# Decode attention on cached pages: fp32 products for four sequences at once on four column groups, in place of split fp32r products one sequence at a time

## The chip, the cores and the metric

The kernel runs on one core of one Trainium2 chip. The metric is the device time of one execution in microseconds (us), the median of several executions. Engines: PE is TensorE's matmul, PEld its weight load, DVE is VectorE, ACT is ScalarE, POOL is GpSimd, SP is SyncE; q behind a name (PEq, SPq) is that engine's queue.

## The reference, cut to what matters

One layer of a hybrid decoder, for a prompt of 2048 positions and for 8 sampled tokens (8 sequences, one new position each, behind 2048 cached positions in pages of 128). The part that is changed is the attention of the 8 sampled tokens over their caches:

```python
def mla_attend(q_abs, q_r, q_pos, ckv, kr, k_pos):
    s = (jnp.einsum('bqhr,bkr->bhqk', q_abs, ckv).astype(jnp.float32)
         + jnp.einsum('bqhp,bkp->bhqk', q_r, kr).astype(jnp.float32)) * SOFTMAX_SCALE
    mask = q_pos[:, None] >= k_pos[None, :]
    s = jnp.where(mask[None, None], s, NEG_INF)
    p = jax.nn.softmax(s, axis=-1).astype(ckv.dtype)
    return jnp.einsum('bhqk,bkr->bqhr', p, ckv)
...
        past_ckv = cache_ckv[l][page_table].reshape(dec_b, past_len, KV_RANK)
        past_kr = cache_krope[l][page_table].reshape(dec_b, past_len, QK_ROPE)
        xs, c_s, k_s, s_s = mixer_layer(xs, past_len, state_pool[l], past_ckv, past_kr, *lw)
```

Here b is 8 sequences, h 8 heads, q one query, k 2048 cached keys and the new one; a latent key (`ckv`, 128 numbers) is also the value, a rotary key (`kr`) has 64 numbers. Everything is float32.

## The kernel before

The program is four stages, each a block that ends when all engines are through: `project` (latents, keys and queries of 17 tiles of 128 positions, the last tile being the sampled tokens), `attend` (the prompt's causal attention, 32 units of 4 heads by 128 queries), `decode` (the sampled tokens' attention) and `merge` (gates and output products, in 5 chunks of 412 tokens). Nothing of one stage runs in another, except what `early_decode` holds: tiles and semaphores that `attend` fills for `decode`.

The prompt's products are made with fp32r operands, each number as a high part (rounded to fp32r) and a low part (the rest), and three products in place of one: high·high, high·low, low·high (L108, and `PARTS` at L911). The high part is an ACT copy, the low part a DVE subtraction (`split`, L78, whose instructions all carry L80).

**In attend.** The order of the instructions of PE, ACT and DVE is planned by `attend_orders` (L504) and is the same list before and after. Ahead of that list DVE makes the row numbers of the cache's pages (L761), clears `q` and `qp_f` (L763, L764), waits for the loads of the decode queries and copies them to `qc_f` and, one group of 8 columns for each sequence in a row of zeros, to `qp_f` (L766, L770). ACT makes their high parts ahead of its first exponential (L733, L734), DVE the low parts ahead of its first normalisation, step P of unit 0 (L814, L815). When POOL has split the last queries it issues the indirect loads of the caches of sequences 0 and 1 (L715; `fetch_cache`, L887).

**In decode.** POOL issues the other six sequences' loads at once, latent cache `cn` (1 MB each) and rotary cache `rn` (0.5 MB) in turn. There are 32 steps, one for each sequence s and each quarter c of its keys (512 keys):

- PE turns four 128x128 tiles of latent keys and two of rotary keys (two 64-number keys side by side) into PSUM with an identity (L1024, L1027);
- ACT copies them out as high parts (L960, L961), DVE subtracts them for the low parts (L980, L982);
- PE makes the scores of the step before (L1008, L1012): 3 + 6 products. The stationary operand is 64 columns wide, with the 8 heads of sequence s in their place and zeros elsewhere, so that all 8 sequences add up in one bank of 64 rows per quarter.

Then follow, one behind the other: the new key's scores (L1038, L1040), five evictions to `sc` with their maxima (L985, L989), one exponential over 64 rows by 2056 (L963), the reciprocal (L995), the normalisation (L997), 17 transposes (L1048, L1050), evictions to `pt` (L965, L999), and the values: for each sequence 17 plain fp32 products with 8 stationary columns (`pt`) and 128 moving ones (the latent cache), L1057 and L1059. PE turns the result (L1064), ACT evicts it, SP stores it (L946), and the block ends.

A plain fp32 product is one instruction of the program and shows as two MATMULs and two LDWEIGHTS in the trace; fp32r products and transposes show as one each.

Of the kernel before, what the change touches and what calls it, by code (L numbers as in the profile page):

```python
# [27 lines left out]
P = 128  # L28
# [3 lines left out]
NDEC = 8  # L32
# [27 lines left out]
SH = NDEC * NH  # L60
SROW = SH + NH
RUN = PAST // P
EARLY = 2
# [549 lines left out]
def attend(nc, io, keep, early):  # L613
# [3 lines left out]
    with ExitStack() as ctx:  # L617
# [3 lines left out]
        def sem(name):  # L621
# [26 lines left out]
        pages, run, rows, q, qc_f, qp_f, qc, qp = (  # L648
            early[name] for name in ("pages", "run", "rows", "q", "qc_f", "qp_f", "qc", "qp"))
        pages_in, rows_ok, dq_in, q_zero, qc_f_ok, qp_f_ok, dq_hi, dq_ok = (  # L650
            early[name] for name in ("pages_in", "rows_ok", "q_in", "q_zero", "qc_f_ok", "qp_f_ok", "q_hi", "q_ok"))
# [49 lines left out]
        def _(pool):  # L701
# [13 lines left out]
            for sequence in range(EARLY):  # L715
                fetch_cache(pool, io, rows, sequence, early["cn"][sequence], early["rn"][sequence],
                            early["cache_in"][sequence])

        @block.scalar
        def _(act):  # L720
            for step in orders["ACT"]:
# [7 lines left out]
                elif kind == "E":  # L729
                    if step == ("E", 0, 0, 0):  # L730

                        act.wait_ge(qp_f_ok, 1)
                        act.activation(qp[:, 0, :, :], qp_f[:, :, :], ACT.Copy).then_inc(dq_hi, 1)  # L733
                        act.activation(qc[:, 0, :, :], qc_f[:, :, :], ACT.Copy).then_inc(dq_hi, 1)  # L734
# [23 lines left out]
        def _(dve):  # L758
# [5 lines left out]
            dve.memset(qp_f[:, :, :], 0.0).then_inc(q_zero, 1)  # L764
            dve.wait_ge(dq_in, 80)
            dve.tensor_copy(qc_f[:, :, :].rearrange("p a (s h) -> p a s h", s=NDEC),  # L766
                            q[:, :, :, :].rearrange("p a h s -> p a s h")).then_inc(qc_f_ok, 1)
            dve.wait_ge(qc_f_ok, 1)
            dve.wait_ge(q_zero, 2)
            dve.tensor_copy(qp_f[:, :, :].rearrange("p a (s c) -> p a s c", s=NDEC)[:, :, :, 0:NH],  # L770
                            qc_f[:, :, :].rearrange("p a (s h) -> p a s h", s=NDEC)).then_inc(qp_f_ok, 1)
            dve.wait_ge(mask_in, 16)
            for step in orders["DVE"]:
# [35 lines left out]
                elif kind == "P":  # L809
                    if step == ("P", 0, 0, 0):  # L810

                        dve.wait_ge(qp_f_ok, 1)
                        dve.wait_ge(dq_hi, 2)
                        split(dve, qp[:, 1, :, :], qp_f[:, :, :], qp[:, 0, :, :]).then_inc(dq_ok, 1)  # L814
                        split(dve, qc[:, 1, :, :], qc_f[:, :, :], qc[:, 0, :, :]).then_inc(dq_ok, 1)  # L815
# [79 lines left out]
def decode(nc, io, keep, early):  # L895
# [5 lines left out]
    with ExitStack() as ctx:  # L901
# [100 lines left out]
        def _(pe):  # L1002
# [14 lines left out]
            for n in range(STEPS):  # L1017
                s, c = n // 4, n % 4
                if c == 0:
                    pe.wait_ge(cache_in[s], 32)  # L1020
# [721 lines left out]
```

## Time and profile before

| | |
|---|---|
| median of 3 runs | 2333.02 us (2332.59 to 2333.3) |
| the profiled execution, its own time | 2344.84 us |
| its span, first to last instruction | 2343.0 us |
| PE busy, share of the span | 2205.3 us, 94% |
| PEld, DVE, ACT, POOL | 87%, 56%, 43%, 16% |
| HBM read, written | 213.45 MB, 42.79 MB |
| project | 0 to about 250 us |
| attend | about 250 to 944 us |
| decode | 949.0 (first instruction of PE) to 1072.1 us (store issued) |
| merge | from 1079.3 us to the end |

Times on the trace are microseconds from the span's start. The windows view gives for each stretch what each engine was busy, with the number of instructions, the mean clock granted to TensorE as a share of 2.4 GHz (0.50 is 1.2 GHz), and the load of the DMA engines. The timeline view merges neighbouring instructions of a kind (x4 is four) and gives in brackets the idle time ahead of them and who ended it. A matmul's own duration holds its way through the array, so back-to-back matmuls are measured by the distance of their starts, not by their durations.

### The profile page before, as it was taken

Reading aid. Unit: us, or ns where it says so; the run is one execution under the profiler, and the core shown is the slowest. Engines: PE = TensorE matmul, PEld = TensorE weight load, DVE = VectorE, ACT = ScalarE, POOL = GpSimd, SP = SyncE. Lnnn points to the kernel's source line nnn. Section 1 sums busy time; section 2 is a strip of 40 time slices with the busy share of each in tenths; the row PEclk is TensorE's granted clock in tenths of the full one; section 3 lists DMA queues with packets and bytes.
Section 4 is the critical chain, followed back from the end, with each engine's and each line's share of the span. In section 5 each row is a group of like instructions: output and inputs, shape, how many; then the busy total and the mean of one; then the engine's idle time right before and its main releaser. Section 6 shows DMA issues by size and latency. Waiting matters only on the chain.

```text
span 2343.0 us, 33629 instructions
## 1 busy us (share of the span) xinstructions
PE 2205.3 (94%) x12021; PEld 2036.9 (87%) x12021; DVE 1308.4 (56%) x2647; ACT 1002.9 (43%) x1802; POOL 364.7 (16%) x500
## 2 busy tenths in 40 slices
PE   5999599999999998786999999999999999999997
PEld 4888478888888887665999999999999999999997
DVE  4565477788777776332644455444644464446445
ACT  3555456555555544322433343334333443344333
POOL 1333221111000010101400050004100420023001
PEclk9999799999999999887999999999999999999999
DMA  5454432111110010404453434443453345344533
GB/s 171 150 162 145 118 81 55 41 35 34 28 28 28 19 64 5 166 1 156 129 176 119 142 118 157 145 137 119 135 166 121 128 136 174 106 150 134 175 117 131
DMA packets 134866, 257.99 MB, mean 110 GB/s; under 512 B 18682, under 2 KB 84482, under 8 KB 133430
## 3 DMA queue, kind: packets, MB, share of 16 engines
q1 hardware_dynamic: 111454, 223.29, 29.3%
q10 hardware_dynamic: 20960, 20.19, 2.9%
q0 software_dynamic: 2304, 12.58, 1.4%
q8 instruction: 88, 1.44, 0.3%
q14 instruction: 60, 0.49, 0.1%
HBM read 213.45 MB, written 42.79 MB: 109 GB/s over the span
## 4 chain that ended last, share of the span: by engine, by line
PE 51%; DVE 1%; issue 1%; DMA 0%; ACT 0%; POOL 0%; DVEq 0%; POOLq 0%; SPq 0%; ACTq 0%
PE d_ps L112 50%; PE d_ps L1567 1%; DMA d_hf<-out_ht 0%; DVE d_gate_p L1518 0%; DVE d_mrg L80 0%; POOL d_fstat L1389 0%; DVE d_y L1481 0%; ACT d_mrg L1347 0%; ACT d_zs L1375 0%; DVE d_ya L1522 0%; DVE d_ht L80 0%; ACT d_ht L1293 0%; DVE d_pool L80 0%; DVE d_y L1556 0%; DVE d_y L1483 0%
## 5 line engine op out<-in xcount | busy, mean ns | idle before, releaser
L112 PE MATMUL d_ps<-d_ht,d_wr 128*128 128x412 f32 x3840 | 737.4, 350 | 22.2 <-DVE d_ht L80 22.1
L112 PEld LDWEIGHTS d_ps<-d_ht,d_wr 128*128 128x128 f32 x3840 | 718.3, 188 | 26.2 <-issue 22.6
L80 DVE TENSOR_TENSOR d_wr<-d_ws,d_wr 128x1024 fp32r<-128x1024 f32 x262 | 322.9, 1232 | 553.4 <-ACT d_wr L1288 553.3
L1288 ACT ACTIVATE d_wr<-d_ws 128x1024 fp32r<-128x1024 f32 x262 | 277.5, 1059 | 608.2 <-PE d_ps L112 598.9
L842 PE MATMUL b_ps<-kt,b_qs 128*128 128x512 f32 (+3 forms) x1600 | 359.8, 377 | 18.6 <-POOL b_qs L80 13.8
L842 PEld LDWEIGHTS b_ps<-kt,b_qs 128*128 128x128 f32 x1600 | 278.3, 195 | 65.2 <-POOL b_qs L80 14.3
L861 PE MATMUL b_ps<-b_pt,kv 128*128 128x512 f32 x816 | 211.5, 402 | 8.7 <-DVE b_pt L80 8.7
L80 DVE TENSOR_TENSOR b_pt<-b_ps,b_pt 128x512 fp32r<-128x512 f32 x272 | 171.9, 683 | 83.0 <-ACT b_pt L746 82.6
L739 ACT ACTIVATE b_p<-b_p,b_bias 128x1024 f32<-128x1024 f32 (+7 forms) x192 | 172.0, 898 | 103.8 <-DVE b_low L797 100.4
L746 ACT ACTIVATE b_pt<-b_ps 128x512 fp32r<-128x512 f32 x272 | 143.8, 596 | 146.6 <-PE b_ps L852 146.3
L861 PEld LDWEIGHTS b_ps<-b_pt,kv 128*128 128x128 f32 x816 | 153.6, 191 | 48.3 <-DVE b_pt L80 14.1
L112 PE MATMUL d_ps<-d_mrg,d_wr 128*128 128x412 f32 x960 | 188.8, 352 | 0.7
L112 PE MATMUL d_ps<-d_gat,d_wr 128*128 128x412 f32 x960 | 186.5, 349 | 0.0
L112 PEld LDWEIGHTS d_ps<-d_gat,d_wr 128*128 128x128 f32 x960 | 179.5, 188 | 0.6
L112 PEld LDWEIGHTS d_ps<-d_mrg,d_wr 128*128 128x128 f32 x960 | 175.8, 188 | 3.7 <-DVE d_mrg L80 2.4
L80 POOL TENSOR_TENSOR b_qs<-b_qf,b_qs 128x512 fp32r<-128x512 f32 x64 | 87.9, 1373 | 519.1 <-ACT b_qs L728 516.5
L852 PE MATMUL b_ps<-ident,b_p 128*128 128x128 f32 x1088 | 137.6, 275 | 14.6 <-DVE b_p L820 14.3
L852 PEld LDWEIGHTS b_ps<-ident,b_p 128*128 128x128 f32 x1088 | 125.7, 142 | 29.1 <-DVE b_p L820 16.9
L790 DVE TENSOR_SCALAR_CACHE_REDUCE b_p<-b_ps 128x512 f32<-128x512 f32 x192 | 130.6, 686 | 35.7 <-PE b_ps L842 27.8
L1411 POOL TENSOR_TENSOR d_win<-d_u 128x426 f32<-128x426 f32 x20 | 21.2, 1062 | 740.8 <-ACT d_u L1330 740.0
L820 DVE TENSOR_SCALAR b_p<-b_p,b_inverse 128x1024 f32<-128x1024 f32 (+7 forms) x192 | 122.9, 670 | 1.4
L112 PE MATMUL a_ps<-a_wlat,a_ht 128*128 128x448 f32 x408 | 89.0, 374 | 6.5 <-DVE a_wlat L80 6.5
(193 smaller groups left out, 2289.4 us busy)
## 6 DMA issues: line engine op xcount, KB each, us to landing
d_ws<-in_w SPq DMA_DIRECT2D x264, 512.0 KB, 3.5
out_q<-a_qout SPq DMA_DIRECT2D x17, 768.0 KB, 3.3
d_hf<-out_ht SPq DMA_DIRECT2D x26, 412.0 KB, 3.5
a_x<-in_x ACTq DMA_DIRECT2D x17, 512.0 KB, 3.8
out_ht<-a_hf SPq DMA_DIRECT2D x17, 512.0 KB, 4.2
d_olf<-out_olat SPq DMA_DIRECT2D x42, 206.0 KB, 2.9
b_qf<-out_q SPq DMA_DIRECT2D x32, 256.0 KB, 2.8
b_qf<-out_q SPq DMA_DIRECT2D x128, 64.0 KB, 2.6
```

The lines of the kernel that those rows point to most:

```text
L80: return e.tensor_tensor(low, source, high.bitcast(f32), ALU.subtract)
L112: mm = pe.matmul(out, stationary(a, k), moving(b, k), start=first and k == 0 and a + b == 0, stop=last and k == depth - 1 and a == 1)
L739: act.activation(sp_[row][:, keys], sp_[row][:, keys], ACT.Exp, bias=bias[:, row:row + 1], scale=SCALE, accum_out=total[:, row, part:part ...
L746: act.activation(pt[n % NPT][:, 0, :], ps_t[n % NTB][:, :], ACT.Copy).then_inc(pt_hi, 1)
L790: dve.tensor_scalar(out, inp, 1.0, None, ALU.mult, ALU.max, accum_out=top[:, row, c:c + 1]).then_inc(s_sb, 1)
L820: dve.tensor_scalar(sp_[row][:, keys], sp_[row][:, keys], inverse[:, row:row + 1], None, ALU.mult).then_inc(p_ok, 1)
L842: mm = pe.matmul(ps_s[n % NS][:, 0:keys * P], q[:, a, h, :], kt[:, first:first + keys, b, :], start=k == 0, stop=k == len(pairs) - 1)
L852: mm = pe.transpose(ps_t[n % NTB][:, h * P:h * P + P], sp_[(u % 2) * HG + h][:, j * P:j * P + P], ident[:, :])
L861: mm = pe.matmul(ps_o[u % 2][:, :], kv[:, j, a, :], pt[n % NPT][:, b, :], start=j == 0 and k == 0, stop=j == tiles(u) - 1 and k == 2)
L1288: act.activation(wr[k % 2][:, 0, :, :], ws[k % 4][:, :, :], ACT.Copy).then_inc(w_hi, 1)
L1411: own(pool.tensor_tensor(out[:, start:HIST + T], source[:, start:HIST + T], source[:, start - shift:HIST + T - shift], ALU.add))
L1567: mm = pe.transpose(bank[xt_bank(n)][0:rows, s * P:s * P + P], yt[n % 2][:, s * P:s * P + rows], ident[:, :])
```

## The change

`decode` is written anew; `early_decode` and a few steps of `attend` change with it.

- **Products.** Queries (`qd`) and keys are plain fp32, no high and low parts. The queries of each sequence stand in 32 stationary columns (8 heads, 24 zeros; `PAD`).
- **Four sequences at once.** A step is one quarter of the keys of four sequences, 8 steps in all. Sequence j of the four writes rows 32j to 32j+31 of the same bank. The calls go round the four sequences: four products of 512 columns, then twice four of 256. The same rows and the same going round hold for the new key's scores and for the values, which have 32 stationary columns now.
- **Copies.** ACT copies the latent keys out of PSUM, DVE the rotary keys, each once. Three banks for turned latent keys, two for rotary.
- **Softmax.** One for each four sequences, over 128 rows. The exponentials are not normalised; the values are, when they are evicted. Of the first four it is placed under the steps of the second four.
- **Memory and loads.** `ckeys` lies where attend's `kv` was. Latents of four and rotary keys of three sequences are loaded in attend (was two and two); decode loads rotary keys 3 first, then four sequences' of both less one.
- **Unchanged:** the reference's outputs, attend's planned order, the other stages.

The core of the diff (the evictions of the softmax and the declarations are left out):

```diff
-EARLY = 2
+QUAD = 4
+PAD = P // QUAD
+EARLY_N, EARLY_R = 4, 3
...
@@ attend, vector, ahead of the planned order @@
-            dve.memset(qp_f[:, :, :], 0.0).then_inc(q_zero, 1)
+            dve.memset(qd[:, :, :, :], 0.0).then_inc(q_zero, 1)
             dve.wait_ge(dq_in, 80)
-            dve.tensor_copy(qc_f[:, :, :].rearrange("p a (s h) -> p a s h", s=NDEC),
-                            q[:, :, :, :].rearrange("p a h s -> p a s h")).then_inc(qc_f_ok, 1)
-            dve.wait_ge(qc_f_ok, 1)
             dve.wait_ge(q_zero, 2)
-            dve.tensor_copy(qp_f[:, :, :].rearrange("p a (s c) -> p a s c", s=NDEC)[:, :, :, 0:NH],
-                            qc_f[:, :, :].rearrange("p a (s h) -> p a s h", s=NDEC)).then_inc(qp_f_ok, 1)
+            dve.tensor_copy(qd[:, :, :, 0:NH], q[:, :, :, :].rearrange("p a h s -> p a s h")).then_inc(dq_ok, 1)
...
@@ decode, gpsimd @@
-            for sequence in range(EARLY, NDEC):
-                fetch_cache(pool, io, rows, sequence, cn[sequence], rn[sequence], cache_in[sequence])
+            for sequence in range(EARLY_R, NDEC):
+                fetch_rotary(pool, io, rows, sequence, rn[sequence], cache_in[sequence])
+                if sequence >= EARLY_N:
+                    fetch_latents(pool, io, rows, sequence, cn[sequence], cache_in[sequence])
...
@@ decode, scalar @@
+            for n in range(STEPS):
+                for j in range(QUAD):
+                    keys(n, j)
+                    if n == CHUNKS and j == QUAD - 1:
+                        exponents(0)
+            turned_exponents(0)
+            exponents(1)
+            turned_exponents(1)
...
@@ decode, tensor @@
+            def columns(g):
+                return [(QUAD * g + j, j, slice(PAD * j, PAD * j + PAD)) for j in range(QUAD)]
+
+            def scores(n):
+                g = n // CHUNKS
+                pe.wait_ge(ckeys_ok, QUAD * n + QUAD)
+                pe.wait_ge(rkeys_ok, QUAD * n + QUAD)
                 if n >= 2:
-                    pe.wait_ge(keys_ok, n - 1)
...
+                    pe.wait_ge(s_sb, n - 1)
+                for s, j, to in columns(g):
+                    pe.matmul(ps_s[n % 2][to, :], qd[:, 0, s, :], ckeys[:, n % 2, j, :], start=True, stop=False)
+                for half in range(2):
+                    for s, j, to in columns(g):
+                        mm = pe.matmul(ps_s[n % 2][to, :].rearrange("q (t a k) -> q t a k", t=2, a=2)[:, :, half, :],
+                                       qd[:, 1 + half, s, :],
+                                       rkeys[:, n % 2, j, :].rearrange("p (t k) -> p t k", t=2),
+                                       start=False, stop=half == 1)
+                mm.then_inc(s_ok, 1)
...
+            def values(g):
+                pe.wait_ge(pt_ok, 5 * g + 5)
+                pe.wait_ge(new_in, 32)
+                for s, j, to in columns(g):
+                    pe.matmul(ps_o[g][to, 0:R], ptn[:, g, to], cnew[:, :], start=True, stop=False)
+                for t in range(RUN):
+                    for s, j, to in columns(g):
+                        mm = pe.matmul(ps_o[g][to, 0:R], pt[g][:, t, to], cn[s][:, t, :], start=False, stop=t == RUN - 1)
+                mm.then_inc(o_ok, 1)
...
+            pe.wait_ge(q_ok, 1)
+            for n in range(STEPS):
+                for j in range(QUAD):
+                    transposes(n, j)
+                    if n >= 1 and j == 0:
+                        scores(n - 1)
+                if n == 0:
+                    new_scores(0)
+                    new_scores(1)
             scores(STEPS - 1)
...
+            turn_exponents(0)
+            values(0)
+            turn_exponents(1)
+            turn_latents(0)
+            values(1)
+            turn_latents(1)
```

**PE, two steps of decode's loop.** Before, one sequence's quarter after another (the first row ends the step before; `c_cn`, `c_rn` caches, `c_ckeys`, `c_rkeys` the turned keys, `e_qp` the queries, `ident` the identity):

```order
L1012 MATMUL c_ps<-c_rkeys,e_qp 64x2x128 x6
L1024 MATMUL c_ps<-ident,c_cn 128x128 x4
L1027 MATMUL c_ps<-ident,c_rn 128x128 x2
L1008 MATMUL c_ps<-c_ckeys,e_qp 64x512 x3
L1012 MATMUL c_ps<-c_rkeys,e_qp 64x2x128 x6
```

After, one step, and its scores behind the first of the next step's transposes (`e_qd` the queries):

```order
L1048 MATMUL c_ps<-ident,c_cn 128x128 x4
L1054 MATMUL c_ps<-ident,c_rn 128x128 x2
L1048 MATMUL c_ps<-ident,c_cn 128x128 x4
L1054 MATMUL c_ps<-ident,c_rn 128x128 x2
L1048 MATMUL c_ps<-ident,c_cn 128x128 x4
L1054 MATMUL c_ps<-ident,c_rn 128x128 x2
L1048 MATMUL c_ps<-ident,c_cn 128x128 x4
L1054 MATMUL c_ps<-ident,c_rn 128x128 x2
L1068 MATMUL c_ps<-c_ckeys,e_qd 32x512 x4
L1071 MATMUL c_ps<-c_rkeys,e_qd 32x2x128 x8
```

For four quarters PE had 24 transposes and 36 fp32r products, in four such pieces; now it has the 24 transposes and 12 plain fp32 products, which are two instructions each.

**PE, from the last scores to the end of decode.** Before (`c_sc` the exponentials, `c_pt` them turned; the last two value rows repeat for eight sequences):

```order
L1008 MATMUL c_ps<-c_ckeys,e_qp 64x512 x3
L1012 MATMUL c_ps<-c_rkeys,e_qp 64x2x128 x6
L1038 MATMUL c_ps<-kt,e_qc 64x8 x3
L1040 MATMUL c_ps<-kt,e_qc 64x8 x3
L1048 MATMUL c_ps<-ident,c_sc 128x64 x16
L1050 MATMUL c_ps<-ident,c_sc 8x64
L1057 MATMUL c_ps<-c_cnew,c_ptn 8x128
L1059 MATMUL c_ps<-e_cn,c_pt 8x128 x16
```

After:

```order
L1068 MATMUL c_ps<-c_ckeys,e_qd 32x512 x4
L1071 MATMUL c_ps<-c_rkeys,e_qd 32x2x128 x8
L1090 MATMUL c_ps<-ident,c_sc 128x128 x16
L1092 MATMUL c_ps<-ident,c_sc 8x128
L1098 MATMUL c_ps<-c_cnew,c_ptn 32x128 x4
L1101 MATMUL c_ps<-e_cn,c_pt 32x128 x64
L1090 MATMUL c_ps<-ident,c_sc 128x128 x16
L1092 MATMUL c_ps<-ident,c_sc 8x128
L1108 MATMUL c_ps<-ident,c_o 128x128
L1098 MATMUL c_ps<-c_cnew,c_ptn 32x128 x4
L1101 MATMUL c_ps<-c_cn,c_pt 32x128 x64
L1108 MATMUL c_ps<-ident,c_o 128x128
```

The new key's scores have left this place for the end of step 0; of the second four sequences the transposes stand behind the values of the first four.

**ACT in decode, after.** Its copies of the keys, with the first four sequences' exponential among them:

```order
L950 ACTIVATE c_ckeys<-c_ps 128x512 x20
L954 ACTIVATE c_sc,c_total<-c_sc,c_bias 128x2056
L950 ACTIVATE c_ckeys<-c_ps 128x512 x12
L960 ACTIVATE c_pt<-c_ps 128x512 x2
L954 ACTIVATE c_sc,c_total<-c_sc,c_bias 128x2056
L960 ACTIVATE c_pt<-c_ps 128x512 x2
L972 ACTIVATE c_o<-c_ps,c_inverse 128x128
```

Before, the 32 pairs of copies stood ahead of the only exponential.

## Rows read from the trace of the kernel before

**Rows 1.** The page: engines' shares, then the granted clock in 40 slices.
```profile
PE 2205.3 (94%) x12021; PEld 2036.9 (87%) x12021; DVE 1308.4 (56%) x2647; ACT 1002.9 (43%) x1802; POOL 364.7 (16%) x500
...
PEclk9999799999999999887999999999999999999999
```

**Rows 2.** Windows of the decode stage; columns stand in the first line.
```profile
core 0: us, PE busy (x) PEld busy (x) DVE busy (x) ACT busy (x) POOL busy (x), PEclk, DMA share, GB/s
...
944.10:949.00 4.90, 0.00 (x0) 0.02 (x1) 0.00 (x0) 0.00 (x0) 0.00 (x0) 0.79 0.19 54
949.00:954.00 5.00, 4.43 (x18) 3.48 (x19) 2.13 (x5) 1.75 (x4) 3.46 (x4) 0.53 0.54 185
...
959.40:964.80 5.40, 0.00 (x0) 0.00 (x0) 1.02 (x2) 0.87 (x2) 3.75 (x4) 0.92 1.02 423
964.80:971.00 6.20, 6.14 (x24) 4.92 (x25) 2.05 (x5) 1.74 (x4) 0.00 (x0) 0.52 1.01 412
971.00:1024.80 53.80, 53.46 (x393) 45.54 (x390) 26.57 (x52) 22.75 (x52) 0.00 (x0) 1.00 0.07 30
1024.80:1036.10 11.30, 3.98 (x32) 3.31 (x32) 4.92 (x15) 2.91 (x4) 0.00 (x0) 0.68 0.00 1
1036.10:1070.50 34.40, 34.31 (x272) 24.38 (x272) 0.00 (x0) 0.61 (x2) 0.00 (x0) 0.91 0.00 1
```

**Rows 3.** Timeline of one step of four key tiles: start, us, engine.
```profile
975.07 0.47 PEld L1024 LDWEIGHTS c_ps<-ident,c_cn 128*128 128x128 f32 x4
...
975.51 0.25 PEld L1027 LDWEIGHTS c_ps<-ident,c_rn 128*128 128x128 f32 x2
...
975.73 0.47 PEld L1008 LDWEIGHTS c_ps<-c_ckeys,e_qp 128*64 128x64 f32 x3
...
976.04 0.60 ACT L960 ACTIVATE c_ckeys<-c_ps 128x512 fp32r<-128x512 f32 x1 [1.17 <-PE c_ps L1027]
976.30 0.83 PEld L1012 LDWEIGHTS c_ps<-c_rkeys,e_qp 128*64 128x64 f32 x6
...
977.12 0.14 PEld L1024 LDWEIGHTS c_ps<-ident,c_cn 128*128 128x128 f32 x1
```

**Rows 4.** Timeline after the last score: softmax, values, the end.
```profile
1029.72 2.01 ACT L963 ACTIVATE c_sc<-c_sc,c_stat 64x2056 f32<-64x2056 f32 x1 [5.74 <-DVE c_low L993]
...
1035.39 0.69 DVE L999 TENSOR_SCALAR c_pt<-c_ps 128x512 f32<-128x512 f32 x1 [2.06 <-PE c_ps L1048]
...
1047.28 3.66 PE L1059 MATMUL c_ps<-c_cn,c_pt 128*8 128x128 f32 x32
...
1072.12 0.57 SPq L946 DMA_DIRECT2D out_olat<-c_olat  x1
```

**Rows 5.** Instructions of line 444: ns min/median/max, first and last start.
```profile
L444 PE MATMUL a_ps<-a_wuk_t,a_wuq_t x32: 275/275/275, 31.9 to 35.4; 128*128 128x128 f32 x32
```

**Rows 6.** Instructions of line 1064, the same columns.
```profile
L1064 PE MATMUL c_ps<-ident,c_o x8: 200/201/227, 1071.1 to 1071.6; 8*128 8x8 f32 x8
```

**Rows 7.** Rotary cache loads issued early, with their landing.
```profile
L891 POOL DMA_INDIRECT e_rn<-in_cache_krope,e_rows x2: 938/981/1024, 845.1 to 847.7; - x2
...
DMA to landing us min/median/max: 8.9/8.9/8.9
```

**Rows 8.** Rotary cache loads issued in the decode stage.
```profile
L891 POOL DMA_INDIRECT c_rn<-in_cache_krope,e_rows x6: 934/938/941, 950.9 to 963.3; - x6
...
DMA to landing us min/median/max: 11.9/12.6/13.2
```

**Rows 9.** Timeline at the start of attend: the decode queries' work.
```profile
267.44 1.64 ACT L733 ACTIVATE e_qp<-e_qp_f 128x1728 fp32r<-128x1728 f32 x1 [6.49 <-DVE e_qp_f L770]
...
275.78 1.96 DVE L80 TENSOR_TENSOR e_qp<-e_qp_f,e_qp 128x1728 fp32r<-128x1728 f32 x1
277.66 1.42 DVE L80 TENSOR_TENSOR e_qc<-e_qc_f,e_qc 128x192 fp32r<-128x192 f32 x1
...
279.92 1.44 PE L852 MATMUL b_ps<-ident,b_p 128*128 128x128 f32 x8 [2.40 <-DVE b_p L820]
```

More of the change, by code:

```diff
@@ L645, in attend @@
         o_out = [sem("o_out0"), sem("o_out1")]
[L648 to L651, printed above, removed]
+        pages, run, rows, q, qd = (early[name] for name in ("pages", "run", "rows", "q", "qd"))
+        pages_in, rows_ok, dq_in, q_zero, dq_ok = (
+            early[name] for name in ("pages_in", "rows_ok", "q_in", "q_zero", "q_ok"))
         orders = attend_orders()
@@ L714, in _ @@
             pool.wait_ge(rows_ok, 1)
[L715 to L717 removed]
+            for sequence in range(EARLY_N):
+                fetch_latents(pool, io, rows, sequence, early["cn"][sequence], early["cache_in"][sequence])
+                if sequence < EARLY_R:
+                    fetch_rotary(pool, io, rows, sequence, early["rn"][sequence], early["cache_in"][sequence])
         @block.scalar
@@ new lines, in decode @@
+        ps_pn, ps_o, ps_ot = bank[6], (bank[7], bank[0]), bank[1]
+        NCT, NRT = len(ps_c), len(ps_r)
+        GROUPS, CHUNKS = NDEC // QUAD, RUN // 4
+        STEPS = GROUPS * CHUNKS
+        rows, qd, cache_in, q_ok = (early[name] for name in ("rows", "qd", "cache_in", "q_ok"))
+        cn = early["cn"] + [sb(f"cn{s}", [P, RUN, R]) for s in range(EARLY_N, NDEC)]
+        rn = early["rn"] + [sb(f"rn{s}", [P, RUN, ROPE]) for s in range(EARLY_R, NDEC)]
+        ckeys = nc.alloc_sbuf_tensor_at("c_ckeys", [P, 2, QUAD, 512], f32, offset=keep["kv_at"])
@@ new lines, in decode @@
+        rkeys = sb("rkeys", [P, 2, QUAD, 2 * P])
+        cnew = sb("cnew", [NDEC, R])
+        own = sb("own", [P, GROUPS, NDEC])
+        sc = [sb(f"sc{g}", [P, PAST + NDEC]) for g in range(GROUPS)]
+        pt = [sb(f"pt{g}", [P, RUN, P]) for g in range(GROUPS)]
+        ptn = sb("ptn", [NDEC, GROUPS, P])
+        o = sb("o", [P, GROUPS, R])
+        top = sb("top", [P, GROUPS, CHUNKS + 1])
+        low = sb("low", [P, GROUPS, CHUNKS + 1])
+        bias, total, inverse = sb("bias", [P, GROUPS]), sb("total", [P, GROUPS]), sb("inverse", [P, GROUPS])
@@ new lines, in new_scores, with turn_exponents @@
+            def new_scores(g):
+                out = slice(NDEC * g, NDEC * g + NDEC)
+                for k, (part, b) in enumerate(((0, 0), (0, 2), (1, 1), (1, 3))):
+                    for s, j, to in columns(g):
+                        mm = pe.matmul(ps_new[to, out], qd[:, part, s, :], kt[:, NT - 1, b, 0:NDEC].bitcast(f32),
+                                       start=k == 0, stop=k == 3)
+                mm.then_inc(new_ok, 1)
+            def turn_exponents(g):
+                pe.wait_ge(exp_ok, g + 1)
+                for n in range(4):
+                    for t in range(4):
+                        at = (4 * n + t) * P
+                        mm = pe.transpose(ps_p(g, n)[:, t * P:t * P + P], sc[g][:, at:at + P], ident[:, :])
+                    mm.then_inc(p_turned, 1)
+                pe.transpose(ps_pn[0:NDEC, 0:P], sc[g][:, PAST:PAST + NDEC], ident[:, :]).then_inc(p_turned, 1)
```

242 lines of the change are left out of this document (107 added, 135 removed).

## The prediction

> **What bounds the kernel now.** I read the page first: PE is busy 94% of the span, and the granted clock is near full except at 4 and at 16 to 18 of the 40 slices [rows 1]; the second dip is the decode stage. The windows cut that stage up [rows 2]: nothing runs on PE from 944.1 to 949.0 (change of stage), the clock is about half (1.2 GHz) for the first 5 us, PE is empty for 5.4 us while the loads fill the DMA engines (423 GB/s), the clock is half again for 6 us, then PE is full for 53.8 us, nearly empty through the softmax, and full for the 34.4 us of the values. From PE's first instruction at 949.0 to the store at 1072.12 [rows 4] it takes 123.1 us, 5% of the run, and PE or what PE waits for sets it all; merge can't start before it ends. The timeline of one step shows the period: 975.07 to 977.12, 2.05 us for one quarter of one sequence, 0.66 of it transposes and 1.39 the nine fp32r products [rows 3]; ACT's copy of 0.60 hides.
>
> **The price of a plain fp32 product.** 32 value instructions (16 products) take 3.66 us, 0.114 each [rows 4]; the 32 of line 444, with 128 stationary columns, start within 35.4 − 31.9 us, 0.113 each [rows 5]. So a pass over 128 columns is 0.114 us whatever the width of the stationary side, and a product is two passes. For 256 and 512 columns nothing is shown; I scale by columns, 0.228 and 0.456. Eight transposes of 8 columns start within 0.5 us of each other, 0.06 to 0.07 each [rows 6]: below 0.06 no pair of load and product goes, however short.
>
> **Whether four column groups overlap** decides the case, and the trace has no two neighbouring products on different groups. Bounds: no overlap, or all four at once. Between them lies what the order allows. Each product is two passes on the same group, and its second can't start before its first has streamed. If PE starts instructions in program order, sequence 1's first pass runs beside sequence 0's second, and then its own second must wait for it: two passes at a time, never four. I take this twofold overlap: it follows from the calls going round by product, not by pass.
>
> The Trainium skill, "TensorE: Matmul & The Clock Gate", Part 3, measures 2.38x for three column tiles and says that matmuls start and end strictly in program order. Nothing here shows an overlap yet; by its span formula alone all four would run together, which is the second rival.
>
> **The sum**, from PE's first decode instruction (0):
> - *To the third load's landing: 11.* PE turns sequences 0 to 2 in some 4 us at half clock, then waits for the rotary keys of sequence 3, issued at 0.6. Landing took 8.9 us with few loads about [rows 7], 11.9 to 13.2 in the full queue [rows 8]; being first I take 10.4. Between 9.5 and 14. This wait stands where the 5.4 us hole stood [rows 2], and the half clock behind it stays.
> - *First transposes and the new key's scores: 6.3.* 6 transposes at half clock 1.3; 32 products of 8 columns, 64 passes, at 0.06 to 0.12: 5. Was 0.4 us of the stretch after 1024.8. To 17.3.
> - *The remaining transposes:* 28 groups of six by 0.66 = 18.5. To 35.8. (As before: 32 by 0.66 in all.)
> - *Scores: 8 steps.* 4·2·0.456 + 8·2·0.228 = 7.3 us one behind the other; halved 3.65, plus 0.15 to fill and drain: 3.8. 30.4, plus 1 for the first at half clock. Before, 32 by 1.39 = 44.5. To 67.2. ACT has 4 by 0.60 a step and DVE about as much, under 6.4 us of PE; ACT's exponential in step 4 hides under the scores of that step.
> - *Turning the exponentials, twice 3.1:* 17 transposes 1.9, then the last eviction (0.69 [rows 4]) and a small one, with nothing for PE. Between 2.6 and 3.6. The exponential (2.01 us [rows 4]), the reciprocal and the normalisation, which filled most of the 11.3 us from 1024.8 [rows 2], lie under other work or are gone.
> - *Values, twice 8.2:* 68 products, 136 passes at the 0.06 floor, which is about half of 0.114. Before 34.4. With the line above 22.6: to 89.8.
> - *The end: 1.5* (1.7 before): 91.3.
>
> So decode takes 91.3 for 123.1, **31.8 less**. At attend's start two DVE splits of 1.96 and 1.42 us stand right before the normalisation for which PE waits 2.40 us [rows 9]; they go. ACT's 1.64 ends before its exponentials, which wait for DVE and PE in between, so I price it at nothing (if uncovered, 2 us). Later attend has PE full, so the lead stays: 2.4 to 5.6, I take **3.0**, between PE's wait and the 3.4 of the splits. Three more loads are issued near attend's end, and nothing in attend waits for them: nothing. What ended the hole at 959.4 no row names; I take it as covered by the wait for the load, and if it comes back behind that it costs up to 5.4.
>
> 34.8 less: the profiled execution goes from 2344.84 to 2310.0. The median lies 11.8 lower and has the same stage, so **2333.0 − 34.8 = 2298.2 us**. Own range 2286 to 2312: the load ±3, the scores from 3.5 to 4.6 us, the passes of the values 0.057 to 0.08, attend ±2.
>
> **Rivals.**
> 1. *No overlap, loads hidden.* Everything else holds, but scores cost 7.3 for 3.8 (+28) and values 136·0.114 = 15.5 for 8.2 (+14.6). Total −34.8 + 42.6 = +7.8: **2341**. For it: no row shows an overlap, and a quarter's plain scores cost 0.91 + 2·0.456 = 1.82 us against 1.39 as nine fp32r products [rows 3]. This is the case on the other side. The point from which it decides: scores and values one behind the other sum to 89 us, so if four neighbours save less than 7.8 of them, about a tenth, the change loses.
> 2. *Fourfold overlap.* Scores at 7.3/4, about 2.0 with filling: −14.4; values stay at the floor of 0.06. **2284**; with values at 0.03 too, 2276. Against it: the two passes of one product on one group.
> 3. *Weight loads that don't hide.* If on split columns each load (24.38/272 = 0.09 us, hidden in the values before [rows 2]) waits for the product in flight, 192 + 272 + 64 = 528 passes pay 0.09 each on top of rival 1: +47, **2388**. Against it: PEld is busy 24.4 of the 34.4 us beside a full PE [rows 2].
> 4. *Half of it:* scores overlap and values don't (+14.6), or the load lands at 20 (+9): **2307 to 2313**.
>
> On rival 3: the same page's Part 3 says a weight load overlaps products in flight only when its row group differs, and here all groups have the same rows. [Rows 2] disagree for one group; for four no run here shows it. "TensorEngine Tiling (Array Packing)", Key Properties, says that a change of tiling drains the engine; transposes and scores alternate 16 times, and the 0.15 a step covers one such drain of the usual 0.16 us between a matmul's duration and its distance.
>
> **Chances.** Forecast 0.57; fourfold 0.16; half 0.07; no overlap 0.13; loads exposed 0.05; the rest 0.02. The range takes the fourfold case and the lower part of the no-overlap case: 2274 to 2337. About 0.2% (4.7 us) is what a measurement here can tell from nothing: faster 0.80, within it 0.06 (no overlap with more saved at the start), slower 0.14.
>
> **What would show it.** In the profile after: the distance of starts of the score instructions, 24 in a step: 3.8 us a step is my case, 2 the fourfold, 7.3 the serial. The values: 136 instructions in 8.2 or in 15.5 us. A wait of PE behind the third group of transposes, ended by a load, at about 5 to 11 us from the stage's start. DVE without its splits at 275.8. Merge and project as before. I am wrong if the scores keep the serial distance, if PE waits for ACT's keys in each step, or if the start takes over 20 us.

## The result and the profile after

The changed kernel took **2271.96 us** (median of 4, 2270.19 to 2276.05) beside 2333.16 for the kernel before on the same chip: ratio 0.9739, 95% interval 0.9722 to 0.9756. That is 61.2 us less. The forecast was 34.8 less, 2298.2, with 2274 to 2337 as the range: the sign was right, the size was not, and the result lies 2 us below the range. The fourfold rival (2284, or 2276 with short values) came nearest.

The page of the changed kernel, engines' shares and the granted clock, which answer to [rows 1]:

```profile
PE 2145.7 (95%) x11994; PEld 1988.4 (88%) x11994; DVE 1289.9 (57%) x2632; ACT 994.0 (44%) x1770; POOL 364.3 (16%) x500
...
PEclk9999799999999999889999999999999999999998
```

Windows of the decode stage after, cut at its own steps (compare [rows 2]): the change of stage, PE's start to the landing of the load that it waits for, first transposes and the new key's scores, transposes and scores, first turning, first values, second turning, second values and end.

```profile
core 0: us, PE busy (x) PEld busy (x) DVE busy (x) ACT busy (x) POOL busy (x), PEclk, DMA share, GB/s
936.30:942.10 5.80, 0.00 (x0) 0.00 (x0) 0.08 (x1) 0.28 (x1) 0.00 (x0) 0.67 0.16 45
942.10:946.90 4.80, 3.62 (x18) 3.40 (x18) 1.28 (x4) 1.79 (x3) 3.39 (x4) 0.68 0.57 154
946.90:949.30 2.40, 2.39 (x80) 2.03 (x81) 0.42 (x1) 0.74 (x2) 1.79 (x3) 1.00 0.98 370
949.30:983.50 34.20, 33.64 (x355) 23.21 (x354) 16.95 (x48) 18.46 (x30) 3.26 (x4) 1.00 0.38 155
983.50:986.60 3.10, 2.11 (x21) 1.79 (x17) 2.36 (x8) 2.37 (x3) 0.00 (x0) 1.00 0.00 0
986.60:990.60 4.00, 3.96 (x136) 3.59 (x136) 0.05 (x1) 0.70 (x2) 0.00 (x0) 1.00 0.02 4
990.60:993.70 3.10, 2.21 (x22) 1.93 (x18) 1.86 (x6) 1.08 (x2) 0.00 (x0) 1.00 0.00 0
993.70:998.80 5.10, 4.38 (x137) 3.72 (x137) 0.30 (x3) 0.37 (x1) 0.00 (x0) 1.00 0.01 3
```

Decode, from PE's first instruction to the store (998.84), takes 56.7 us. The clock is below full only in the first two windows (0.67 and 0.68); there is no hole and no second cold stretch. The timeline of PE after shows the parts (columns: start, us, engine, line, operation, out<-in, tiles, count, idle before and what ended it):

```profile
942.13 1.08 PE L1048 MATMUL c_ps<-ident,e_cn 128*128 128x128 f32 x4 [6.18 <-PEq L617]
...
946.91 0.66 PE L1048 MATMUL c_ps<-ident,e_cn 128*128 128x128 f32 x4 [1.17 <-DMA c_rn<-in_cache_krope,e_rows]
...
947.72 0.82 PE L1081 MATMUL c_ps<-kt,e_qd 128*32 128x8 f32 x64
948.47 0.66 PE L1048 MATMUL c_ps<-ident,e_cn 128*128 128x128 f32 x4
...
953.93 1.06 PE L1068 MATMUL c_ps<-c_ckeys,e_qd 128*32 128x512 f32 x8
954.78 1.07 PE L1071 MATMUL c_ps<-c_rkeys,e_qd 128*32 128x256 f32 x16
955.79 0.66 PE L1048 MATMUL c_ps<-ident,e_cn 128*128 128x128 f32 x4
...
983.54 1.97 PE L1090 MATMUL c_ps<-ident,c_sc 128*128 128x128 f32 x16
...
986.64 0.42 PE L1098 MATMUL c_ps<-c_cnew,c_ptn 8*32 8x128 f32 x8 [1.02 <-DVE c_ptn L1009]
986.99 3.70 PE L1101 MATMUL c_ps<-e_cn,c_pt 128*32 128x128 f32 x128
990.62 1.97 PE L1090 MATMUL c_ps<-ident,c_sc 128*128 128x128 f32 x16
```

A pass, here and below, is one of the two MATMULs that make a plain fp32 product. One step's scores for four sequences (24 passes) run from 953.93 to 955.79, 1.86 us; the forecast said 3.8, and 7.3 for passes one behind the other. The values take 3.7 us for 128 passes, 0.029 each, where one pass alone takes 0.114 [rows 4, 5]: half of what I held to be the floor.

**Where the time went.** The first profile of before had an odd stretch that its median doesn't have (below, e1_before), so I compare with the profile of e1_before. Its span is 2331.3, that of the change 2268.4, 62.9 less: decode 113.07 (946.40 to 1059.47) to 56.71, −56.4; attend from its first product to decode's start 686.70 to 683.87, −2.8; the change of stage behind the store 6.25 to 5.84, −0.4; project −1.4 and merge −1.9, which the change doesn't touch and which differ as much between executions of one kernel (attend's first product stands at 258.3 in one execution of the change and at 260.6 in another, e8_after).

The 56.4 us of decode split up by PE's own rows. In e1_before:

```profile
1014.70 0.28 PE L1038 MATMUL c_ps<-kt,e_qc 128*64 128x8 f32 x3
...
1021.83 1.97 PE L1048 MATMUL c_ps<-ident,c_sc 64*128 64x64 f32 x16 [6.67 <-DVE c_sc L997]
...
1024.58 0.59 PE L1057 MATMUL c_ps<-c_cnew,c_ptn 8*8 8x128 f32 x2 [0.68 <-DVE c_pt L999]
```

Transposes and scores took 68.3 us (946.40 to 1014.70) and take 41.4 (942.13 to 983.54), 26.9 less. The new key's scores and the softmax took 7.1; the new key's scores now stand among the 41.4, and PE no longer waits for a softmax: 7.1 less. The turning of the exponentials took 2.75 and takes 6.2, 3.4 more, since there are two. Values and end took 34.9 and take 9.1, 25.8 less.

### The profile page after: what moved, and what is told of

It is laid out like the page before. It is cut to its first block, busy times and chain, and to the rows that moved or that the text cites. A ratio compares the mean times of both kernels' runs of the same rounds, so it can differ in the third digit from the quotient of the medians.

```text
span 2268.4 us, 33558 instructions
## 1 busy us (share of the span) xinstructions
PE 2145.7 (95%) x11994; PEld 1988.4 (88%) x11994; DVE 1289.9 (57%) x2632; ACT 994.0 (44%) x1770; POOL 364.3 (16%) x500
## 4 chain that ended last, share of the span: by engine, by line
PE 53%; DVE 1%; issue 1%; DMA 0%; ACT 0%; POOL 0%; DVEq 0%; POOLq 0%; SPq 0%; ACTq 0%
PE d_ps L112 52%; PE d_ps L1627 1%; DMA d_hf<-out_ht 0%; DVE d_gate_p L1578 0%; DVE d_mrg L80 0%; POOL d_fstat L1449 0%; DVE d_y L1541 0%; ACT d_mrg L1407 0%; ACT d_zs L1435 0%; DVE d_ya L1582 0%; DVE d_ht L80 0%; ACT d_ht L1353 0%; DVE d_pool L80 0%; DVE d_y L1616 0%; DVE d_y L1543 0%
## 5 line engine op out<-in xcount | busy, mean ns | idle before, releaser
L827 PE MATMUL b_ps<-kt,b_qs 128*128 128x512 f32 (+3 forms) x1600 | 359.0, 377 | 18.4 <-POOL b_qs L80 14.6
```

The source lines that it names most:

```text
L827: mm = pe.matmul(ps_s[n % NS][:, 0:keys * P], q[:, a, h, :], kt[:, first:first + keys, b, :], start=k == 0, stop=k == len(pairs) - 1)
```

## The experiments

**1. e1_before: before, unchanged, with a profile of its own.**

> The kernel before, unchanged, profiled again. The first profile of it took 2344.8 us where the median is 2333. If the hole at 959.4 and the half clock behind it were a thing of that one execution, decode takes some 112 us here in place of 123.1 and the span is near 2331. If they belong to the kernel, decode takes 123 again and the extra 11.8 us stand in project or attend.

2332.78 us (2331.43 to 2334.51), ratio 0.9993, interval 0.9983 to 1.0002. Windows of its decode stage at the place that answers to the hole of [rows 2]:

```profile
958.40:960.40 2.00, 2.00 (x16) 1.72 (x15) 1.02 (x2) 0.83 (x3) 1.66 (x2) 1.00 0.98 406
960.40:962.40 2.00, 2.00 (x16) 1.75 (x15) 1.02 (x2) 0.86 (x2) 0.93 (x1) 1.00 1.05 430
```

No hole, full clock, and decode is 113.1 us instead of 123.1. The 5.4 us hole and the 6 us of half clock behind it don't belong to the kernel as such: this profile of it has neither (more in experiment 7).

**2. e2_by_sequence: the products called sequence by sequence.**

```
-                for half in range(2):
-                    for s, j, to in columns(g):
+                    for half in range(2):
...
-                for t in range(RUN):
-                    for s, j, to in columns(g):
+                    for t in range(RUN):
```

> The changed kernel, with scores and values called sequence by sequence (all products of sequence 0, then of 1, ...) in place of going round the four. Theory A (column groups take their products independently, whatever stands between): as the changed kernel, 1.9 us of scores a step, 2272 us. Theory B (PE starts products in program order and only neighbours on different groups overlap, as the prediction had it): 7.3 us a step and 15.5 us for each group's values, some +43 for the scores and +24 for the values, 2335 to 2340 us. Between: a window of so many instructions that the scores' 24 passes of a step overlap in part and the values' 34 of a sequence hardly.

2315.61 us, ratio 0.9922, interval 0.9905 to 0.9938: 43.7 above the change's 2271.96 (another set of runs, in which before took 2335.0 for 2333.16). Timeline of PE, one step's scores, then two of the four sequences' values:

```profile
978.36 1.04 PE L1068 MATMUL c_ps<-c_ckeys,e_qd 128*32 128x512 f32 x2
979.24 0.38 PE L1070 MATMUL c_ps<-c_rkeys,e_qd 128*32 128x256 f32 x1
979.25 0.62 PE L1068 MATMUL c_ps<-c_ckeys,e_qd 128*32 128x512 f32 x1
979.46 0.59 PE L1070 MATMUL c_ps<-c_rkeys,e_qd 128*32 128x256 f32 x2
...
1007.73 0.40 PE L1097 MATMUL c_ps<-c_cnew,c_ptn 8*32 8x128 f32 x2 [1.02 <-DVE c_ptn L1009]
1008.06 3.68 PE L1099 MATMUL c_ps<-e_cn,c_pt 128*32 128x128 f32 x32
1011.67 0.40 PE L1097 MATMUL c_ps<-c_cnew,c_ptn 8*32 8x128 f32 x2
```

A step's scores take 4.5 us (978.36 to 982.86) for 1.86. The second sequence starts at 979.25, 0.89 behind the first: two of the first one's six passes have gone, and four are left (L1070), one running and three waiting. These three come before the second sequence's in the program, but start behind its first, from 979.46 on: a pass that waits for its own group is overtaken. The values take 3.94 us for each sequence, nothing overlaps. What goes on PE between two sequences there is a product of 8 rows, another tiling; in experiment 6 the second four sequences' values differ in this alone (all four such products ahead of the first sequence) and take 13.3 us with these products, where here they take 15.8. So the order of the calls does decide, but not in the way that the prediction had it.

**3. e3_one_tile: the same plain fp32 products on one tile of 128 columns** (queries padded with zeros to 128 columns, no column groups; the wider copy of the queries takes DVE some time at the start).

```
-                    pe.matmul(ps_s[n % 2][to, :], qd[:, 0, s, :], ckeys[:, n % 2, j, :], start=True, stop=False)
+                    pe.matmul(ps_s[n % 2][:, :], qw[:, 0, s, :], ckeys[:, n % 2, j, :], start=j == 0, stop=False)
```

> The changed kernel without column groups: the queries of each sequence stand in 128 stationary columns, zeros but for its own 8, and all four add up in one full bank; the values are 128 wide into one quarter of a bank each, four copies take them out. A copy of the queries to the wide form, about 3 us, is added at decode's start. This prices plain fp32 without overlap: both theories expect 7.3 us of scores a step and 15.5 for each values, 2335 to 2342 us. If it is under 2300, the gain does not come from the groups.

2357.76 us, ratio 1.0102, interval 1.0085 to 1.0118: 1% slower than before. Timeline of PE, a step's scores and one of four sequences' values:

```profile
976.53 3.67 PE L1087 MATMUL c_ps<-c_ckeys,c_qw 128*128 128x512 f32 x8
980.04 3.62 PE L1090 MATMUL c_ps<-c_rkeys,c_qw 128*128 128x256 f32 x16
...
1044.88 3.84 PE L1120 MATMUL c_ps<-e_cn,c_pt 128*128 128x128 f32 x32
```

Scores 6.97 us a step (7.3 was the serial price), values 16.6 (15.5). This is rival 1's mechanism, and it prices the column groups: 8 steps by 5.1 us and two groups' values by 12.6 are 66 of the 86 us that part the two kernels; another 13 are the new key's scores (13.7 us at half clock for 0.8), and PE waits 1.8 us for the wide queries. The overlap is worth 66 us, more than the 61 that the change gains: without it the scores and values would take 89 us (8 by 6.97 and 2 by 16.6) where the split fp32r products before took 79 (44.5 and 34.4). That the whole kernel is 23 us slower than before says less, since the 13 and the 1.8 are this version's own; less these it would be some 8 us slower, an estimate. Split fp32r products on four column groups were not run, so how much of the gain hangs on plain fp32 stays open: the overlap might help them as well.

**4. e4_loads: early loads as before** (`EARLY_N, EARLY_R = 2, 2` for `4, 3`).

> The changed kernel with the caches of two sequences loaded early, as in the kernel before, in place of four latents and three rotary keys. If the early loads matter, PE waits in step 0 for sequences 2 and 3, about 8 to 12 us from the stage's start, with the half clock behind it: +6 to +12 us, 2278 to 2284. If the wait is short because first loads land within 5 us, +2.

2282.18 us, ratio 0.9779, interval 0.9763 to 0.9796: 10.2 above the change. PE's waits in the first 20 us of decode:

```profile
PE c_ps L1048 <- DMA c_cn<-in_cache_ckv,e_rows: 9.1, 2, 6.9
PE c_ps L1048 <- PEq L617: 5.5, 1, 5.5
```

9.1 us of waiting stand where the change has 1.17, and the clock is half behind them; decode takes 66.9 us. The three more loads that are issued early (seven in place of four) are worth 10 us. In e4_loads the latent load that is issued second, at 943.17, ends PE's wait only at 951.11; in the change the rotary load that is first in the queue landed 4.3 us after its issue (942.60 to 946.9), not 10.4.

**5. e6_query_work: e4_loads, with the old work on the decode queries put back at attend's start** (ACT's two copies, DVE's reordering and its two splits; nothing reads them).

> The kernel of e4_loads (two early latent loads and two early rotary loads, everything else as in the change), with the old work on the decode queries put back where it stood at attend's start: DVE's reordering copy, ACT's two copies and DVE's two splits of 1.96 and 1.42 us. Nothing reads their result. Theory 1, the splits stand in front of the normalisation that PE waits for: PE's wait before the first exponentials' transposes goes from 0.5 back to about 2.4 us, and the time is 2.4 to 3.4 us above e4_loads' 2282.2, so 2285. Theory 2, the splits are covered and the 2.9 us that the stretch from attend's first product to decode lost come from elsewhere (the absent loads or executions that differ): same time as e4_loads within 1 us.

2289.11 us, 6.9 above e4_loads (another set of runs; decode is alike, 66.7 and 66.9 us). PE's timeline and the window behind it, e6_query_work:

```profile
278.09 1.97 PE L849 MATMUL b_ps<-ident,b_p 128*128 128x128 f32 x8 [2.50 <-DVE b_p L817]
...
278.86:288.86 10.00, 9.86 (x52) 8.94 (x50) 5.81 (x39) 6.57 (x19) 2.57 (x2) 0.76 0.45 110
```

and e4_loads:

```profile
275.83 1.44 PE L837 MATMUL b_ps<-ident,b_p 128*128 128x128 f32 x8 [0.55 <-DVE b_p L805]
...
278.66:288.66 10.00, 7.11 (x44) 6.08 (x43) 7.06 (x44) 8.03 (x24) 4.40 (x4) 1.00 0.64 120
```

The wait is as expected, 2.50 for 0.55. The rest is the clock. Attend starts at half clock in all these profiles; in e4_loads it is full from shortly after the wait (1.00 over the window above), in e6_query_work PE goes on at half clock some 6 us past the wait (0.76 over its window), and a second dip follows (0.77 from 303.9 to 318.9, 1.00 in e4_loads). Attend up to decode takes 690.0 against 682.8 us. The second dip is not the query work's: e1_before, which has that work, doesn't show it (1.00) and takes 686.7. The five runs lie between 2285.4 and 2289.6 and those of e4_loads between 2279.8 and 2285.4: that the work costs time is shown, whether it is 3 us or 7 is not.

**6. e5_runs and e11_long_runs: how long may the calls stay at one group?** In the values alone, runs of 2 and 4 rows (4 and 8 passes on one group) in e5_runs, of 8 and 16 rows in e11_long_runs (the pair in the first line of the diff).

```
+                span = (2, 4)[g]
+                for first in range(0, RUN, span):
...
+                        for t in range(first, first + span):
```

> The product of each value row is two passes of 0.107 us on one column group, and in the change the calls go round the four sequences after every row. Here, in the values alone, the calls stay longer at a sequence: two rows in a row (4 passes on one group) in the first group of four sequences, four rows in a row (8 passes) in the second. Nothing else is changed. Theory 1, PE has a few waiting places and a pass that waits for its own group holds back only what comes after some three more: runs of two still overlap fully, 3.7 to 4.1 us for the first group's values; runs of four don't, some 6 to 8 us for the second; the run as a whole 2 to 4 us longer than the change, 2274 to 2276. Theory 2, every column group has a queue of its own, deep enough for all: both stay at 4.0 us and the time at 2272. Theory 3 (that of the prediction), strict order of the program: the longer the run the less overlap, more than 8 us for the first and some 13 for the second, 2285.

> As e5_runs, with longer runs: eight rows in a row (16 passes on one column group) in the values of the first four sequences, all sixteen rows of a sequence (32 passes) in those of the second. In e5_runs a block of 8 passes cost 0.50 us, 4.4 passes of 0.114: the next group's passes begin when about 3.6 of the group before are left. If that number does not depend on the length of the run, the first values take 8 blocks by 12.4 passes by 0.114 = 11.3 us and the second 3 by 28.4 + 32 passes by 0.114 = 13.4. If it grows with the run (some share of it overlaps), both stay near 8 us. If all overlap is lost with such runs, as between the sequences of e2_by_sequence, both take 4 by 32 by 0.114 = 14.6.

e5_runs took 2280.18 us (2275.21 to 2280.63), e11_long_runs, run once, 2302.57. Timeline of PE, e5_runs, first and second group of four sequences:

```profile
992.46 3.77 PE L1103 MATMUL c_ps<-e_cn,c_pt 128*32 128x128 f32 x128
...
999.61 8.06 PE L1103 MATMUL c_ps<-c_cn,c_pt 128*32 128x128 f32 x128
```

e11_long_runs:

```profile
1001.36 11.31 PE L1103 MATMUL c_ps<-e_cn,c_pt 128*32 128x128 f32 x128
...
1016.05 12.94 PE L1103 MATMUL c_ps<-c_cn,c_pt 128*32 128x128 f32 x128
```

Same 128 passes: 3.70 us in runs of 2 passes (the change), 3.77 in runs of 4, 8.06 of 8, 11.31 of 16, 12.94 of 32; serially 14.6. One rule gives all five within 4%: a group takes **four passes, one running and three waiting**; while they stand, those for other groups start at once; the fifth holds up everything behind it. A run of p passes then costs (p − 4) times 0.114 before the next group starts, and the last run all of its passes: 7.8 us for p = 8 (16 runs), 11.4 for 16, 13.2 for 32, and nothing lost up to 4. The three times by themselves give 3.7 passes in place of 4. The rule gives e2's scores as well: six passes a sequence, a new sequence every 0.89 us, 4.5 in all. That the waiting passes are counted for each group, and not for all groups together, follows from runs of 4, where twelve passes wait and nothing is lost, beside runs of 16 and 32, where by these times again only some four are left when the next group starts. A strict order of starts (theory 3 of e5_runs: "more than 8 us" for runs of 4) is out.

Of the 8 us by which e5_runs lies over the change, 4.4 are in decode (61.1 for 56.7); 2.8 are in attend (686.6 for 683.9) and come from no edit (see below, on attend's start).

**7. e7, e8, e9, e10, e12: the wait behind the turnings, and the hole.** The change waits 1.02 and 0.91 us for the last evictions of the turned exponentials. e7_turn_inside moves the second turning into the first values; e9_quarters lets the values start with the quarter that is evicted first and puts the new key's product last:

```
-                pe.wait_ge(pt_ok, 5 * g + 5)
+                for n, (ready, count) in ((0, (pa_ok, 2 * g + 1)), (2, (pt_ok, 3 * g + 1)),
+                                          (1, (pa_ok, 2 * g + 2)), (3, (pt_ok, 3 * g + 2))):
+                    pe.wait_ge(ready, count)
```

> The change with the turning of the second four sequences' exponentials moved from behind the first four's values into the middle of them. PE keeps its 17 transposes and their evictions, but the last eviction of the second turning (about 1.2 us with nothing for PE) now lies under the second half of the values. Theory 1, that wait is on the path: decode goes from 56.7 to about 55.6 us, the run 1 us down to 2271, which only the trace can tell. Theory 2, the four evictions are late inside as well, or the break of the values costs as much as is gained (a few tenths for draining twice more): 2272, no difference. If it is more than 1 us slower, the softmax of the second four isn't ready that early.

> The change itself once more, on the chip of these runs, so that the three others are compared with it side by side: 2272 us within 2, decode from PE's first instruction to the store in 56.7 us within 0.5. A larger difference would say that the landing of the first rotary load (4.3 us from its issue) is not the same from one execution to another.

> The change with the values no longer waiting for all five evictions of the turned exponentials: they begin with the four rows that ACT evicts first and wait for one quarter at a time (rows 0, 2, 1, 3 of the quarters), and the product of the new key, which needs the small eviction that ends last, comes at the end in place of the start. Theory 1, the last evictions are what PE waits for behind each turning (1.02 and 0.91 us in the change): each turning goes from 3.1 to about 2.1 us, decode from 56.7 to 54.8, the run 2 us down from e10_after's. Theory 2, the first eviction is late too, or the waits between the quarters cost: decode stays at 56 or above and the time within 1 us of the change.

> The change itself, on the same chip as e9_quarters: 2272 us within 2, decode 56.7 us within 0.2.

e7_turn_inside took 2271.88 us and e8_after, the change on the same chip, 2272.74; decode 56.6 and 56.7 us. No gain that the times can tell: the 0.9 us of wait saved come back as a new wait (0.47 for the eviction of the first output, which the turning used to hide), its transposition, and the break of the values.

e9_quarters took 2279.56 us (2279.37 to 2281.59) and e10_after 2284.06 (2283.79 to 2286.32), where before took 2343.28. PE's timeline of e9_quarters:

```profile
994.25 1.97 PE L1091 MATMUL c_ps<-ident,c_sc 128*128 128x128 f32 x16
...
996.26 3.70 PE L1101 MATMUL c_ps<-e_cn,c_pt 128*32 128x128 f32 x128
...
1000.24 1.97 PE L1091 MATMUL c_ps<-ident,c_sc 128*128 128x128 f32 x16
```

The turnings take 2.0 and 2.1 us instead of 3.1, decode 63.5 against 65.6 in e10_after: the 2 us expected. The other 2.5 us of the distance are attend's start again (683.8 against 686.7), which no edit touches. Its ratio is 0.9733 (0.9720 to 0.9746) beside 0.9752 (0.9739 to 0.9765) for the change in the same set; the intervals overlap, and the change itself had 0.9735 and 0.9739 in other sets, so only the 2 us in the traces are shown.

But in that set the change is 11 to 12 us slower than in the others, and before 8 to 10. PE's timeline and waits in e10_after say where most of it lies:

```profile
951.70 0.55 PE L1081 MATMUL c_ps<-kt,e_qd 128*32 128x8 f32 x39
952.76 0.17 PE L1081 MATMUL c_ps<-kt,e_qd 128*32 128x8 f32 x1 [0.51 <-issue]
953.47 0.27 PE L1081 MATMUL c_ps<-kt,e_qd 128*32 128x8 f32 x3 [0.53 <-issue]
...
PE c_ps L1081 <- issue: 5.5, 7, 1.8
```

After 39 of the 64 short passes PE runs one to four of them at a time, 0.7 us or a multiple of it apart, for 7.4 us, and goes on at half clock; it waits for nothing that the profile shows, while the loads move some 370 GB/s. The load alone doesn't explain it: the change's own profile has the same 370 GB/s over these passes, and no hole. In the first profile of before PE had one wait of the same 5.5 us and the same kind (issue), in the same part of the stage. A twelfth run asked whose it is:

> The kernel of e9_quarters once more, in another set of runs. In e9_quarters' set PE waited for nothing that the profile shows (5.5 us in all) in the middle of the new key's scores, in the change too, and the kernel before took 2343 in place of 2333 us: the same 5.5 us hole as in the first profile of before. Theory 1, the hole belongs to the chip or the execution and not to the change: where before takes 2333 again, this kernel has no hole, decode takes 54.7 us (63.5 less the hole and the half clock behind it), and the time is 2270 us, 2 below the change in such a set. Theory 2, the hole comes with the code of e9_quarters: it is here again whatever before takes.

2279.63 us, ratio 0.9743 (0.9729 to 0.9756), with before at 2341.93: the hole is there again (5.2 us), decode 63.6. Theory 1's condition (before at 2333) didn't come up, so this run doesn't separate the two; but e10_after has the hole and e8_after, the same kernel on another chip, has none, and of the two profiles of before one has it and one has not. The hole goes with the chip or the execution. In decode it costs the change 8.9 us (65.6 for 56.7) and before 10.0 (123.1 for 113.1), so the ratio hardly moves. That e9_quarters takes 2270 us without it was not seen.

## Why the prediction was wrong

Its own sum, against the change's trace (us):

| term | forecast | measured |
|---|---|---|
| to the third load's landing | 11.0 | 4.8 |
| first transposes, new key's scores | 6.3 | 1.6 |
| other transposes and 8 scores | 49.9 | 35.1 |
| turning, twice | 6.2 | 6.2 |
| values twice, and the end | 17.9 | 9.1 |
| decode | 91.3 | 56.7 |
| attend's start | −3.0 | −2.8 |

- **The step that failed** is "If PE starts instructions in program order, sequence 1's first pass runs beside sequence 0's second, and then its own second must wait for it: two passes at a time, never four." A second pass that waits for its own group does not keep the next group's first pass from starting: up to three may wait (e2_by_sequence, e5_runs, e11_long_runs). In the change, line 1068 alone, in windows of 0.1 us (columns: PE, PEld, granted clock, DMA share, GB/s):

```profile
953.90:954.00 0.10, 0.07 (x4) 0.10 (x8) 1.00 0.79 328
954.00:954.10 0.10, 0.10 (x4) 0.08 (x8) 1.00 0.88 369
...
954.20:954.30 0.10, 0.10 (x4) 0.00 (x0) 1.00 1.28 533
954.30:954.40 0.10, 0.10 (x8) 0.00 (x0) 1.00 0.87 369
...
954.60:954.70 0.10, 0.10 (x4) 0.00 (x0) 1.00 0.82 328
```

  Four passes run from 953.93, one of each sequence, and the other four from about 954.37. All eight weight loads are done in 0.2 us, so rival 3 is out too. The scores were forecast at 31.4 us and took 14.9 (8 by 1.86); with the rest of their row in the table, 20.2 for 18.5, this makes 14.8 of the 34.6 us. I had the right rival (fourfold) and gave it 0.16, because I reasoned from an order of starts that no row showed. That its 2276 comes within 4 us of the result is partly luck: its decode (91.3 less 14.4 and 8.2, 68.7) is 12 us too long, mostly by the landing and the new key's scores (below), and the stage that it is taken from is 10 us too long, and the two nearly cancel. The Trainium skill, "TensorE: Matmul & The Clock Gate", Part 3, says that matmuls start strictly in program order; the windows, e2_by_sequence and e5_runs disagree where a pass waits for its own column group. Its 2.38x for three column tiles is 0.79 of the number of tiles; here four give 3.7x (6.97 us of e3_one_tile against 1.86), 0.94 of it.
- **The values** hung on a floor of 0.06 us taken from transposes of 8 columns [rows 6], which run on one tile of 128 columns. On four groups a pass of 128 columns costs 0.029 and one of 8 columns 0.012 (0.75 us for 64). The floor held for that row's tiling, not for PE. This term and the end were 8.8 us too long, 0.4 of it the end.
- **The new key's scores**: 1.6 for 6.3, the same error of floor. The clock was full where I had it at half, but that is the smaller part: at half clock (0.50, e4_loads) the same 64 passes take 0.97 us.
- **The landing**: 4.3 us after the issue for 10.4, and the term 4.8 where I had 9.5 as the lower bound: [rows 7, 8] are loads with others before or beside them, and the bound for the first in the queue should have gone lower. 6.2 us.
- **The base** was wrong in the other direction. "The median lies 11.8 lower and has the same stage" doesn't hold: the first profile had 10 us in decode (113.1 against 123.1) that the runs of the median didn't. I took a hole that no row explained as something to save. Against the stage without the hole my 91.3 saves 21.8, not 31.8. So a sum that was 34.6 us too long missed the saving by 24.6 only; the forecast of the time missed by 26.2, and the 1.6 between the two lies outside decode or between executions.
- **Right**: the turnings to the tenth; the transposes; attend's start; the price of a product (e3_one_tile: 6.97 for 7.3, 16.6 for 15.5), and with it that the change loses without an overlap (2357.8; I had 2341, short mainly by that version's own wide queries and slow new key's scores).

The 2.8 us at attend's start need a caution. PE's wait before its first transposes there was 0.51 us in the profile of the change, nothing to 0.6 in e2, e3, e4, e7, e8, e9 and e12, and attend up to decode took 682.8 to 684.1 us; in e5, e10 and e11 the wait was 1.1 to 1.8, the clock lower over the ten us from these transposes on (0.83 in e5, 0.71 in e10, 0.82 in e11, 0.98 in the change), and it took 686.5 to 686.7, as much as in e1_before, with not one instruction of attend changed. So a gain of 2.8 us there is a gain of one of two courses, and not every run of the change has it.

## What to carry to other kernels

Where small stationary tiles sit on different column groups of PE, call them round by group: here up to four passes (two fp32 products) in a row on one group cost nothing, eight doubled the time (8.06 us for 3.77), and a product of another tiling between them ended the overlap. Before splitting fp32 into fp32r terms, ask what plain fp32 costs on four groups at once: here 1.86 us for the scores of four quarters, against 5.56 for split products one at a time (4 by 1.39) and 6.97 for plain ones. And before forecasting from one profiled execution that lies above the median, find the stretch that makes it longer and take it out of the base; a wait that no row explains is not yet a saving.

## What the runs showed that I had not expected

- By these times a column group of PE holds four passes, one running and three waiting, and others pass them by (3.77, 8.06, 11.31 and 12.94 us for runs of 4, 8, 16 and 32 passes).
- Passes of 8 columns on four groups start 0.012 us apart at full clock and 0.015 at half (e4_loads); on one tile of 128 columns 64 of them took 13.7 us at half clock, 0.214 each (e3_one_tile).
- The half clock with which attend starts lasted longer where PE waited longer before its first transposes: in e10_after (wait of 1.75 us) the clock is 0.71 over the next ten us, in e8_after (0.23), the same kernel, 0.96, and attend takes 2.6 us more. It is no rule for short waits: in decode the change waits 1.17 us, and the clock behind it is 1.00.
- In some executions or on some chips PE receives short passes one to four at a time, some 0.7 us apart, while the loads fill the DMA engines: 5.2 to 5.6 us of hole in five profiles (the first of before, e9, e10, e11, e12), none in the other nine, in the kernel before and in the change alike. What makes the difference was not found.
